# Order of TensorE's jobs at the end of the mixers and in the router of a two-layer decoder trunk

## The reference

```
h = x @ w_in                                  # one projection, cut into the parts below
y_a = short gated convolution (512)           # branch a
y_b = chunked gated linear attention, 4 heads # branch b: rms_norm(o, norm_g) * silu(r)
y_c = latent attention, 4 heads               # branch c
merged = sigmoid(gt_a) * (y_a @ wb_a) + sigmoid(gt_b) * (y_b @ wb_b) + sigmoid(gt_c) * (y_c @ wb_c)
x = layer_norm(alpha * x + merged @ w_o)
# router: 8 groups, 8 experts in each
grp = x @ w_grp + b_grp ; g = argmax(grp) ; p_g = softmax(grp)[g]
top 2 of (x @ w_exp + b_exp)[g] ; weights = p_g * softmax(top 2)
y = sum over the two experts e of  weight * (silu(x @ w_gate[e]) * (x @ w_up[e])) @ w_down[e]
x = layer_norm(alpha * x + y)
x = layer_norm(alpha * x + sigmoid(x @ w_ple_gate + b) * (p @ w_ple_up))
```

## Time and profile before

| | |
|---|---|
| median of 3 runs | 1660.83 us (1656.87 to 1661.82) |
| span of the profiled execution | 1658.9 us (the page gives no other time of it) |
| TensorE busy | 1372.0 us, 83% |
| VectorE, ScalarE busy | 301.5 us, 268.3 us |
| chain that ended last | TensorE 58%, DMA 34%, ScalarE 3%, VectorE 2% |
| DMA | 503.59 MB, mean 304 GB/s |
| layer 0: ybT, wo00, gather | start at 153.6, 283.3, 336.6 us |

### The profile page before, as it was taken

The page is one execution under the profiler, slowest core; times in us unless marked ns, Lnnn a source line. Parts: engine busy times, 40 slices in busy tenths (PEclk is TensorE's granted clock), DMA queues, the critical chain, the costliest instruction groups (busy, mean ns, idle before and its releaser), DMA issues.

```text
span 1658.9 us, 22642 instructions
## 1 busy us (share of the span) xinstructions
PE 1372.0 (83%) x9351; PEld 881.8 (53%) x9351; DVE 301.5 (18%) x715; ACT 268.3 (16%) x432; POOL 24.0 (1%) x90
## 2 busy tenths in 40 slices
PE   7999999988667676767999999998877767677687
PEld 3687887454334343344456878855443434334343
DVE  4232011511000000000532220115010000000025
ACT  1311000212111111100213110003111112111011
POOL 1000000000000000000000000000000000000000
PEclk9999999899989889889999999998998989989899
DMA  9532456259999999999774234723799999999990
GB/s 318 188 141 102 152 214 250 119 208 425 425 424 425 425 425 424 425 424 418 284 260 152 102 115 152 304 114 152 304 424 425 425 424 425 426 425 424 424 416 36
DMA packets 105020, 503.59 MB, mean 304 GB/s; under 512 B 15058, under 2 KB 18052, under 8 KB 54916
## 3 DMA queue, kind: packets, MB, share of 16 engines
q1 hardware_dynamic: 104228, 500.70, 74.7%
q10 hardware_dynamic: 736, 2.11, 0.4%
HBM read 501.73 MB, written 1.05 MB: 303 GB/s over the span
## 4 chain that ended last, share of the span: by engine, by line
PE 58%; DMA 34%; ACT 3%; DVE 2%; issue 1%; SPq 1%; POOL 0%; ACTq 0%; POOLq 0%; DVEq 0%
DMA ring<-in_w_down 32%; PE ps L615 17%; PE ps L1022 10%; PE ps L685 6%; PE ps L919 5%; PE ps L630 5%; PE ps L1032 3%; PE ps L1001 2%; ACT scratch L1243 2%; DMA x<-in_w_up 2%; PE ps L657 1%; PE ps L988 1%; SPq L483 1%; PE ps L1069 1%; PE ps L953 1%
## 5 line engine op out<-in xcount | busy, mean ns | idle before, releaser
L615 PE MATMUL ps<-xT,ring 128*128 128x256 f32 x1280 | 281.6, 381 | 0.0
L1022 PE MATMUL ps<-ring,scratch 128*32 128x512 f32 x1024 | 173.4, 839 | 108.6 <-DMA ring<-in_w_down 104.6
L615 PEld LDWEIGHTS ps<-xT,ring 128*128 128x128 f32 x1280 | 244.8, 192 | 34.4 <-issue 1.0
L1001 PE MATMUL ps<-ring,scratch 128*32 128x256 f32 x2048 | 178.0, 386 | 30.1 <-DMA x<-in_w_up 17.2
L1001 PE MATMUL ps<-scratch 128*32 128x256 f32 x1792 | 173.5, 380 | 20.2 <-DVE scratch L1682 13.8
L1022 PEld LDWEIGHTS ps<-ring,scratch 128*32 128x32 f32 x1024 | 45.2, 147 | 215.2 <-issue 213.8
L1032 PE MATMUL ps<-scratch 128*128 128x512 f32 x256 | 118.4, 605 | 36.9 <-ACT scratch L1243 36.9
L1001 PEld LDWEIGHTS ps<-ring,scratch 128*32 128x32 f32 x2048 | 99.4, 111 | 74.2 <-issue 41.6
L988 PEld LDWEIGHTS ps<-scratch,xT 128*128 128x128 f32 x1024 | 122.3, 196 | 24.6 <-issue 24.1
L988 PE MATMUL ps<-scratch,xT 128*128 128x128 f32 x1024 | 122.7, 279 | 8.6 <-issue 8.6
L1001 PEld LDWEIGHTS ps<-scratch 128*32 128x32 f32 x1792 | 100.8, 110 | 54.5 <-issue 25.7
(11 more groups left out here) (253 smaller groups left out, 941.4 us busy)
## 6 DMA issues: line engine op xcount, KB each, us to landing
ring<-in_w_down SPq DMA_DIRECT2D x128, 1024.0 KB, 18.3
scratch<-in_w_gate SPq DMA_DIRECT2D x80, 1024.0 KB, 24.0
ring<-in_w_up SPq DMA_DIRECT2D x80, 1024.0 KB, 26.7
ring<-in_w_in SPq DMA_DIRECT2D x48, 1024.0 KB, 7.3
ring<-in_w_gate SPq DMA_DIRECT2D x48, 1024.0 KB, 25.0
scratch<-in_w_up SPq DMA_DIRECT2D x32, 1024.0 KB, 25.8
x<-in_w_up SPq DMA_DIRECT2D x16, 1024.0 KB, 26.0
ring<-in_w_br SPq DMA_DIRECT2D x12, 1024.0 KB, 5.2
```

Of the source, the lines that this page charges most:

```text
L615: ins = mm(out[:, m * SEQ:m * SEQ + SEQ], w[k // per][:, k % per, m * 128:m * 128 + 128], rhs[:, k, :], start=(k == 0), stop=(k == nk - 1))
L1001: ins = mm(ps[32 * j:32 * j + 32, 2, i * 256:i * 256 + 256], xgT[:, k, 32 * j:32 * j + 32], w[j][:, k, :], start=(k == 0), stop=(k == K - 1))
L1022: ins = mm(ps[32 * j:32 * j + 32, n, :], hT[:, c, 32 * j:32 * j + 32], w[j][:, c, n * 512:n * 512 + 512], start=(c == 0), stop=(c == 1))
```

## The change

1. ybT is computed behind br_a0 and not ahead of gate_a0, with a flush at its first transpose. ScalarE copies it out behind the first sigmoid.
2. wo00 starts when three of the four sums that go into sig_used are done; the wait for the fourth lies between its fourth and fifth matmul.
3. acc0 is computed ahead of logits(0), acc1 right behind logits(1), both with a flush. alpha_ident is made behind the last sigmoid. ScalarE's permuted(0) comes behind xT_low of tile 1.
4. The places in PSUM: from gate_a1 to x1T0_hi the pairs are as before; gate_a0 has the pair 3, br_a0 0, ybT 1; logit0 3 (which was wo11's), x1T1 0 and 1, logit1 0, rank 1.
5. Idle matmuls: one new ahead of logits(1), two instead of four ahead of rank, one instead of two ahead of the first gather.

```diff
@@ JOBS
-        "yc", "ybT"]
+        "yc"]
...
         JOBS += [f"gate_{_b}{_h}", f"br_{_b}{_h}"]
-JOBS += ["wo00", "wo01", "wo10", "wo11", "x1T0_lo", "x1T0_hi", "x1T1_lo", "x1T1_hi",
-         "logit0", "logit1", "none", "none", "rank", "none", "acc0", "acc1"]
+        if (_b, _h) == ("a", 0):
+            JOBS += ["ybT"]
+JOBS += ["wo00", "wo01", "wo10", "wo11", "x1T0_lo", "x1T0_hi", "none", "logit0", "x1T1_lo", "x1T1_hi", "none", "none",
+         "logit1", "rank", "none", "none", "none", "none", "acc0", "acc1"]
...
-IDLE = {"first LayerNorm": 6, "router": 4, "first P": 2, "hidden": 4, "second LayerNorm": 6}
+IDLE = {"first LayerNorm": 6, "second tile": 1, "router": 2, "first P": 1, "hidden": 4, "second LayerNorm": 6}
@@ TensorE
-                wait_read(pe, "glao", L)
-                start_job("ybT", L)
-                for h in range(GH):
-                    for t in range(T):
-                        o = h * SEQ + t * 128
-                        ins = pe.transpose(pair("ybT")[:, o:o + 128], rs[:, t, h, :], ident[:, :])
-                end_job("ybT", ins)
+                def yb_transposes():
+                    wait_read(pe, "glao", L)
+                    start_job("ybT", L)
...
+                            if h == 0 and t == 0:
+                                flush(ins)
+                    end_job("ybT", ins)
...
                         pe_release(1)
-
-                pe.wait_ge(sig_used, 4 * L + 4)
+                        if h == 0 and b == "a":
+                            yb_transposes()
+
+                pe.wait_ge(sig_used, 4 * L + 3)
                 wo = [f"wo_{i}" for i in range(4)]
-                tm_quarter("wo00", wo, merged, L, 0, 0)
+                tm_quarter("wo00", wo, merged, L, 0, 0, lambda: pe.wait_ge(sig_used, 4 * L + 4))
...
-                logits(0)
-                transposes_of_x("x1T", 1, L, 1)
-                logits(1)
-
-                once(pe, "alpha_ready", L)
-                for t in range(T):
+                def begin_acc(t):
                     start_job(f"acc{t}", L)
                     pe.wait_ge(xfinal, xT_turn(L, 1, t))
                     for n in range(2):
                         ins = mm(half(f"acc{t}", n), alpha_ident, x[:, t, 512 * n:512 * n + 512],
                                  start=True, stop=True, skip_group_check=True)
-                ins.then_inc(ev["acc_begun"], 1)
+                        if n == 0:
+                            flush(ins)
+                    return ins
+
+                once(pe, "alpha_ready", L)
+                begin_acc(0)
+                logits(0)
+                transposes_of_x("x1T", 1, L, 1)
+                keep_clock(ps[:, 7, :].rearrange("p (a n) -> p a n", a=4), IDLE["second tile"])
+                logits(1)
+                begin_acc(1).then_inc(ev["acc_begun"], 1)
@@ ScalarE
-                copy_out("ybT", L, ybT.rearrange("p a n -> p (a n)"), pair("ybT"))
-
...
                         done(name, act.activation(sig[n % 2].rearrange("p a n -> p (a n)"), pair(name), ACT.Sigmoid))
+                        if n == 0:
+                            copy_out("ybT", L, ybT.rearrange("p a n -> p (a n)"), pair("ybT"))
                         n += 1
+                act.mul(alpha_ident, ident[:, :], ALPHA).then_inc(ev["alpha_ready"], 1)
...
-                wait_full(act, "wo11", L)
-                act.mul(alpha_ident, ident[:, :], ALPHA).then_inc(ev["alpha_ready"], 1)
+                xT_low("x1T", L, 1, vecT[:, 17:33])
                 permuted(0)
-                xT_low("x1T", L, 1, vecT[:, 17:33])
                 permuted(1).then_inc(ev["xp_ready"], 1)
```

More of the change, by code:

```diff
@@ L895, in _ @@
                 end_job("yc", ins)
-                wait_read(pe, "glao", L)
-                start_job("ybT", L)
-                for h in range(GH):
-                    for t in range(T):
-                        o = h * SEQ + t * 128
-                        ins = pe.transpose(pair("ybT")[:, o:o + 128], rs[:, t, h, :], ident[:, :])
-                end_job("ybT", ins)
+                def yb_transposes():
+                    wait_read(pe, "glao", L)
+                    start_job("ybT", L)
+                    for h in range(GH):
+                        for t in range(T):
+                            o = h * SEQ + t * 128
+                            ins = pe.transpose(pair("ybT")[:, o:o + 128], rs[:, t, h, :], ident[:, :])
+                            if h == 0 and t == 0:
+                                flush(ins)
+                    end_job("ybT", ins)
                 for b in BRANCHES:
```

## The result

The changed kernel takes a median of 1629.4 us (1627.39 to 1630.92, 4 runs) beside 1660.5 us (1656.87 to 1661.82, 4 runs) of the kernel before: ratio 0.9817, 95% interval 0.9802 to 0.9831, 31.1 us less. The forecast was 1630.9. The span of the profiled execution is 1626.4 us, 32.5 less than in the earlier trace rows.

A forecast was written before the change was run, and what follows sets the result against it. Weight stream bounds the experts, restarted by TensorE's work; TensorE bounds from the experts' end to the next gather. Gains of 11.7 + 8.8 + 9.4 = 29.9 us take the median from 1660.8 to 1630.9 us, range 1623 to 1640 (8 in 10).

The forecast's parts named there:

- The bound: Experts: the weight stream sets the pace, restarted by slots TensorE's work frees; from experts' end to next gather, TensorE bounds.
- Part 1: Mixers: ybT behind br_a0 saves a 3.80 us wait and low clock behind it, 5.4 and 6.3, together 11.7 us.
- Part 2: Output projection: wo00's first half before the last merge saves 2.67 us wait and 1.7 low clock per layer, 8.8 us.
- the clock's 1.7: Projection's first quarter: 1.7 us of its time over a steady quarter is the low clock after TensorE's idle time.
- Part 3: Router: acc0 ahead, faster transposes and logits(1), no VectorE wait for rank: 4.7 us per layer, 9.4 us.
- VectorE's step from rank to the gather: Router's end: kept at 2.36 us in the forecast although an idle matmul leaves it.
- the 5.1 of the bound: Router: gain of 5.1 us per layer instead of 4.7 if the last idle matmul's place counts too.
- the four weight loads behind w_o: Loads into the w_o slots behind logits(0)'s flush: start 0.65 us late, without consequence.
- rival B: Router: the clock falls around rank in both layers, 3 us each, gain 23.9, 1637 us; chance 0.15.
- C: Only the mixers' gain arrives, the router's goes into another wait: gain 20.5 us, 1640 us; chance 0.06.
- D: Nothing arrives: the stream is bound by its amount and starts as before, 1661 us; chance 0.04.
- E: Low clock from the router through the whole first group in both layers: 8.7 us slower, 1669.5 us; chance 0.03.

The follow-up runs named there:

- experiment 8: Changed kernel with the third group's four gate loads issued ahead of the second group's four down loads in SyncE's queue: 1617.1 us, ratio 0.9748.
- experiment 9: As experiment 8, and besides the fourth group's gate loads ahead of the third group's down loads: 1611.13 us, ratio 0.9716.
- experiment 4: Kernel before, order and waits kept, with four idle matmuls ahead of ybT's wait and three ahead of wo00's: 1652.57 us, ratio 0.9961.
- experiment 5: Kernel before, order kept, only fewer idle matmuls: 2 for 4 ahead of rank, 1 for 2 ahead of the first gather: 1655.02 us, ratio 0.9972.
- experiment 7: Changed kernel with acc0 back behind logits(0), ahead of acc1: 1631.7 us, ratio 0.9833.
- experiment 6: Changed kernel with no idle matmul at the second tile, ahead of rank and ahead of the first gather: 1631.31 us, ratio 0.983.
- experiment 1: Kernel before with only ybT moved behind br_a0, with its flush and ScalarE's copy: 1648.07 us, ratio 0.9935.
- experiment 2: Kernel before with only the wait for the last merge moved to the middle of wo00: 1648.54 us, ratio 0.9931.
- experiment 3: Kernel before with only the changes behind wo11: job order, places in PSUM, idle counts, ScalarE's order: 1648.6 us, ratio 0.9935.
- experiment 10: The changed kernel itself timed once more, beside experiment 9: 1628.81 us, ratio 0.9823.

## Why the prediction was right

**The bound.** Right and now shown twice: the saturated stretch kept its length while its start moved by 16.3 us, and in experiments 8 and 9 the stream restarted earlier with no change on TensorE, and the end followed by what the next stops of the stream left of it (4.4 of 9.4 us in layer 0 of experiment 8).

**Part 1.** 5.4 and 6.3 us were forecast, 5.6 and 6.5 came. Its split into the wait and the clock is confirmed by experiment 4: the clock's share was forecast at 1.6 and 2.5 us, and 1.6 and 2.5 came.

**Part 2.** 4.4 per layer were forecast, 4.6 came; of the clock's 1.7 experiment 4 shows 1.6 and 1.7. The sum was ready 0.8 us before its new wait, as worked out, so nothing took the wait's place.

**Part 3.** 4.7 per layer were forecast, 5.4 and 5.3 came. The under-sized term is VectorE's step from rank to the gather, which I had kept at 2.36 us; without the second idle matmul it is 321.97 - 320.16 = 1.81. I had named that as part of the 5.1 of the bound and not taken it. The other terms came as forecast: counted from wo11's transposes (309.03 before, 299.74 now), the reading of the logits and the weights each lie within 0.2 us of the schedule. Two small terms were off without consequence: 3.60 / 8 is 0.45 us a pass and not 0.43 (acc0 took 1.80 us to the next start), and the four weight loads behind w_o started 1.5 us later in that count and not 0.65.

Of the router's 5.3 us some 2.2 are the fewer idle matmuls (experiment 5), the rest are faster transposes and logits. The text let acc0 ahead carry the clock for both; experiment 7 shows that one layer of two comes without it. Logits(1) took 3.66 us in all ten layers that had neither acc0 ahead nor the new idle matmul, 1.98 in both layers with the idle matmul alone (experiment 7), and 2.60 and 1.98 with acc0 ahead alone (experiment 6). So either of the two does most of it. The new order of ScalarE's work was not tried by itself.

**The clock as a danger** (rival B) did not come in the changed kernel: the gather took 3.84 us in both layers. But B was a real danger, and a part of it is there at the new counts of idle matmuls. In the traces with the old counts (kernel before, experiments 1, 2 and 4) the first gather took 3.73 us in all eight layers; in those with the new counts (changed kernel, experiments 3, 5, 7, 8, 9, 10) it took 3.84 in eleven of fourteen and 5.27, 4.46 and 5.14 in layer 0 of experiments 3, 7 and 9. With no idle matmul (experiment 6) it took 6.8 and 6.1 us. The sentence of the Trainium skill named beside B (TensorE: Matmul & The Clock Gate, "What's actually happening") was right in its direction: these traces agree, with a granted clock of 0.64 in experiment 6's router window where the changed kernel had 1.00. That both layers of the changed kernel escaped it is in part luck.

**What was not in the sum** is the first group: 1.6 us in layer 0 that the down matmuls took less. In this set the stretch from the gather to the restart (kernel before, changed kernel, experiments 1 to 5 and 7), wherever the gather had its full pace, is 18.1 to 18.4 us in seven layers and 19.8 to 20.0 in seven, whatever the edit, so I call it chance of the moment. With the 0.9 us lost ahead of yc and 0.1 in layer 1 it is 0.6 of the 2.6 us between the span's 32.5 and the forecast's 29.9; the other 2.0 are the sizes of the three parts, above all VectorE's step. **C, D and E** did not come: the stretch kept its length and moved by all that TensorE gave.

## What to carry to other kernels

Find first what restarts the saturated stretch, and follow each microsecond to that event; here it was the release of four slots, and once it was known, issuing two groups of four loads ahead of others gave 18 us, over half of what three careful edits of TensorE's order gave. In this kernel a wait of 2.7 or 3.8 us on TensorE had two prices, its length and the low clock of the work behind it; moving a job behind 20 us of independent work saved both, filling the wait with useless matmuls saved the second alone (7.4 of 21.3 us). Idle matmuls paid where they ended about when the wait did (experiments 4 and 6); those that outlasted it were delay (experiment 5). And compare two traces stretch by stretch between the same marks: a difference of spans also holds stretches that no edit touches.

## What the runs showed of the hardware beyond that

Work that no edit touches changed its duration with its place in time: the same 32 down matmul passes took 3.64 or 5.34 us, the same eight transposes 1.04 to 1.94, between kernels and between the two layers of one run, along with the granted clock (1.00 and 0.68 over the down matmuls of the changed kernel's two layers). The two profiles of the changed kernel, taken on different occasions, agreed in these durations within 0.2 us. Why the pattern repeats for one program and not between neighbours is left open.
